# Projection loop turned by three tiles, a new stage for x, and another order behind the last tile

## The reference, cut to what matters

```python
u = rmsnorm(h, norm_mix[i])
z = u @ w_in[i]                                   # 2048 -> 3360 + 3072 + 16
z_rw, z_fox = z[..., :N_SHIFT], z[..., N_SHIFT:]
z_prev = jnp.pad(z_rw, ((0, 0), (1, 0), (0, 0)))[:, :-1]
z_rw = z_rw + (z_prev - z_rw) * mu_shift[i]       # token shift
...
r, k, v, xw, xa, xg = jnp.split(z, RWKV_SPLITS, axis=-1)
w_log = -jax.nn.softplus(-(w0 + jnp.tanh(xw) @ w2)) - 0.5
decay = jnp.exp(-jnp.exp(w_log.astype(f32)))
a = jax.nn.sigmoid(a0 + xa @ a2)
kk = kk / jnp.maximum(jnp.sqrt(jnp.sum(kk * kk, axis=-1, keepdims=True)), 1e-12)
k = k * (1.0 + (a - 1.0) * k_a)
# a scan over 512 steps of a 64x64 state per head, with r, decay, k, v, kk, a
bonus = jnp.sum(r_h * k_h * r_k.astype(f32), axis=-1, keepdims=True) * v_h
...
logits = jnp.einsum('bhqd,bhkd->bhqk', q_blk, kh).astype(f32) * scale
logits = logits + (c_blk[..., None] - c[:, :, None, :])   # causal, per block of 128
probs = jax.nn.softmax(logits, axis=-1)
out = jnp.einsum('bhqk,bhkd->bhqd', probs.astype(vh.dtype), vh)
```

## Time and profile before

| what | value |
|---|---|
| median of 3 runs | 2836.48 us (2836.39 to 2837.19) |
| time of the profiled execution | 2838.68 us |
| its span | 2837.0 us |
| TensorE busy | 2745.4 us (97%) |
| VectorE, ScalarE, GpSimd busy | 1244.4, 882.0, 165.9 us |
| mean granted TensorE clock | 0.981 |
| DMA, mean over the span | 109 GB/s |

### The profile page before, as it was taken

The page is one execution under the profiler, slowest core; times in us unless marked ns, Lnnn a source line. Parts: engine busy times, 40 slices in busy tenths (PEclk is TensorE's granted clock), DMA queues, the critical chain, the costliest instruction groups (busy, mean ns, idle before and its releaser), DMA issues.

```text
span 2837.0 us, 46091 instructions
## 1 busy us (share of the span) xinstructions
PE 2745.4 (97%) x17826; PEld 2190.1 (77%) x17826; DVE 1244.4 (44%) x1635; ACT 882.0 (31%) x1300; POOL 165.9 (6%) x172
## 2 busy tenths in 40 slices
PE   8999999999779899999999999999999999999997
PEld 5867777777458867888888888888888888888886
DVE  4365555665524454544322343223432243334444
ACT  4244444444334432422211222112221122223233
POOL 0000000000023200200000000000000000011110
PEclk9999999999879999999999999999999999999998
DMA  6444555454352233333333333333333333333333
GB/s 183 125 132 141 149 149 145 119 148 130 95 167 93 82 104 89 96 97 96 96 96 96 96 96 96 96 96 96 96 96 96 97 97 97 96 97 105 99 93 91
DMA packets 533117, 309.64 MB, mean 109 GB/s; under 512 B 56365, under 2 KB 508613, under 8 KB 532045
## 3 DMA queue, kind: packets, MB, share of 16 engines
q1 hardware_dynamic: 484093, 275.83, 33.8%
q10 hardware_dynamic: 43552, 14.71, 1.9%
q0 software_dynamic: 5424, 18.45, 1.7%
HBM read 272.64 MB, written 36.31 MB: 109 GB/s over the span
## 4 chain that ended last, share of the span: by engine, by line
issue 56%; PE 36%; DVE 2%; POOL 2%; DMA 2%; ACT 1%; SPq 0%; DVEq 0%; POOLq 0%; ACTq 0%
PE acc L563 6%; PE acc L565 6%; PE acc L564 6%; PE acc L913 2%; PE acc L914 2%; PE acc L915 2%; POOL sumsq L1867 2%; PE bank L647 1%; PE bank L634 1%; PE bank L717 1%; PE bank L727 1%; PE bank L662 1%; PE acc L727 1%; DMA w_raw<-in_w_in 1%; PE bank L640 1%
## 5 line engine op out<-in xcount | busy, mean ns | idle before, releaser
L1405 DVE TENSOR_TENSOR w_lo<-w_raw,w_hi 128x1024 fp32r<-128x1024 f32 (+1 forms) x422 | 522.5, 1238 | 1172.3 <-ACT w_hi L1041 1170.8
L1041 ACT ACTIVATE w_hi<-w_raw 128x1024 fp32r<-128x1024 f32 x420 | 444.8, 1059 | 1225.4 <-PE acc L565 1161.2
L563 PE MATMUL acc<-a_hi,w_hi 128*128 128x512 f32 x1824 | 719.5, 394 | 4.4 <-DVE w_lo L1405 4.3
L565 PE MATMUL acc<-a_hi,w_lo 128*128 128x512 f32 x1824 | 711.6, 390 | 0.0
L564 PE MATMUL acc<-a_lo,w_hi 128*128 128x512 f32 x1824 | 711.4, 390 | 0.0
L563 PE MATMUL acc<-b_hi,w_hi 128*128 128x512 f32 x1280 | 498.5, 389 | 0.0
L565 PE MATMUL acc<-b_hi,w_lo 128*128 128x512 f32 x1280 | 498.0, 389 | 0.0
L564 PE MATMUL acc<-b_lo,w_hi 128*128 128x512 f32 x1280 | 498.0, 389 | 0.0
L563 PEld LDWEIGHTS acc<-a_hi,w_hi 128*128 128x128 f32 x1824 | 343.3, 188 | 89.9 <-issue 18.7
L565 PEld LDWEIGHTS acc<-a_hi,w_lo 128*128 128x128 f32 x1824 | 343.2, 188 | 71.8
L564 PEld LDWEIGHTS acc<-a_lo,w_hi 128*128 128x128 f32 x1824 | 343.3, 188 | 71.1 <-issue 1.7
(11 more groups left out here) (267 smaller groups left out, 2151.2 us busy)
## 6 DMA issues: line engine op xcount, KB each, us to landing
w_raw<-in_w_ff SPq DMA_DIRECT2D x256, 512.0 KB, 4.0
w_raw<-in_w_in SPq DMA_DIRECT2D x100, 512.0 KB, 3.8
w_raw<-in_w_out SPq DMA_DIRECT2D x32, 512.0 KB, 3.9
w_raw<-in_w_ple_gate SPq DMA_DIRECT2D x32, 512.0 KB, 3.9
z_d<-ev POOLq DMA_DIRECT2D x50, 256.0 KB, 3.4
ab_d<-ab ACTq DMA_DIRECT2D x8, 1024.0 KB, 7.0
x_c<-ab_d SPq DMA_DIRECT2D x8, 1024.0 KB, 4.9
x_t<-ab_d SPq DMA_DIRECT2D x9, 512.0 KB, 3.9
```

Of the source, the lines that this page charges most:

```text
L563: mm(dst, wh, hi[:, kt, :], start=kt == 0, stop=False)
L565: last = mm(dst, wl, hi[:, kt, :], start=False, stop=kt == KT - 1)
L1041: A(w_hi[:, s, :, :], w_raw[:, s, :, :], ACT.Copy).then_inc(sg("w_hi_ready"), 1)
L1405: V.tensor_tensor(w_lo[:, s, :, 0:width], w_raw[:, s, :, 0:width], w_hi[:, s, :, 0:width].bitcast(F32), ALU.subtract).then_inc(sg("w_split ...
```

## The change

What it does:

- The order of a pair's tiles is k, q, fox k, fox v, r, v. The loop starts after the third tile of a pair (`Z_LEAD = 3`), so a turn computes fox v, r and v of pair i and k, q, fox k of pair i+1, with the side work of pair i beside them. The last three tiles of the eighth pair come behind the loop with steps 1 to 5 beside them (`last_side`), and the once-only steps stand in the first three tiles.
- `load_pair` loads k, q and fox k, and waits for the store of the third tile of the pair. Fox v, r and v are loaded by themselves, each two tiles after its own.
- Beside the tiles, VectorE's receptance (shift of r) moves from step 2 to 6, the values (shift of v, bonus) from 3 and 7 to 8, the features to 7; ScalarE's store of `ab` moves to step 7, those of v and the bonus to 9. Two operations of VectorE per pair are merged into others. `pr` has a buffer for each head.
- Behind the last tile VectorE does receptance and features first, then values, and head 1's softmax last.
- In the x stage the narrow product is made block by block (`narrow`), its weights have a buffer of their own, the first unit is loaded and split inside the stage, h is stored by quarters as they are ready, and four blocks of squares are added up by four matmuls of 32 columns that write different partitions.

```diff
-Z_COLUMNS = (DR, 0, 2 * DR, N_SHIFT, N_SHIFT + DR, N_SHIFT + 2 * DR)
+Z_COLUMNS = (DR, N_SHIFT, N_SHIFT + DR, N_SHIFT + 2 * DR, 0, 2 * DR)
+Z_LEAD = 3
...
             def load_pair(i):
-                sp.wait_ge(sg("ev_free0"), i * 48 + 80)
+                sp.wait_ge(sg("ev_free0"), i * 48 + 64)
...
-                sp.wait_ge(sg("ev_free1"), i * 48 + 64)
+                sp.wait_ge(sg("ev_free1"), i * 48 + 48)
...
                 sp.wait_ge(sg("side_inputs_used"), i + 1)
-                for t, dst in enumerate((kin, rin, vin, qin, k_in)):
...
+                for t, dst in enumerate((kin[:, 1:], qin[:, :], k_in[:, :])):
+                    load_tile(i, t, dst, "side_landed")
...
             with sp.Fori(0, NPAIR - 1) as i:
                 for t in range(Z_PAIR):
-                    pair_units(i, 2 + Z_PAIR + t, t)
+                    pair_units(i, 2 + Z_LEAD + t, (Z_LEAD + t) % Z_PAIR)
                     if t == 0:
                         load_pair(i)
-                    if t == 1:
+                    if t == 2:
                         load_fox_v(i)
+                    if t == 3:
+                        load_receptance(i)
+                    if t == 4:
+                        load_value(i)
...
-            def sum_squares(f):
-
-                pe.wait_ge(sg("squares_ready"), f + 1)
-                mm(bank[3][:, :], ones, sq[:, f % 2, :], start=f == 0, stop=f == KT - 1).then_inc(sg("x_squares_summed"), 1)
+            def sum_squares(g):
+
+                pe.wait_ge(sg("squares_ready"), NB * g + NB)
+                for j in range(NB):
+                    last = mm(bank[3][32 * j:32 * j + 32, :], const(C_ONE, 32), squares[j], start=g == 0, stop=g == H_X - 1)
+                last.then_inc(sg("x_squares_summed"), 1)
+
+            def narrow(k):
...
+                mm(bank[0][0:48, :], nw_hi[:, k, :], a_hi[:, k, :], start=k == 0, stop=False)
+                mm(bank[0][0:48, :], nw_hi[:, k, :], a_lo[:, k, :], start=False, stop=False)
+                return mm(bank[0][0:48, :], nw_lo[:, k, :], a_hi[:, k, :], start=False, stop=k == KT - 1)
...
+            i = NPAIR - 1
+            pair_tiles(i, 2 + Z_LEAD, last_side, Z_LEAD)
+            pe.wait_ge(sg("logits_max_ready"), i * 8 + 4)
+            logits(i, 1)
+            pe.wait_ge(sg("fv_ready"), i + 1)
+            pe.wait_ge(sg("acc_taken"), 2 + Z_TILES)
+            sum_bonus(i, acc[1])
+            transpose_probs(i, 0, last_prob_banks)
+            weigh_values(i, 0)
+            transpose_probs(i, 1, last_prob_banks)
+            weigh_values(i, 1)
...
+            def store_values(i):
+
+                act.wait_ge(sg("bonus_taken"), i + 1)
+                act.dma_start(v_d[:, :, bass.ds(i, 1), :].rearrange("p c a t -> p c (a t)"), vs[:, :].rearrange("p (c t) -> p c t", c=NC)).then_inc(sg("features_stored"), 16)
+                act.dma_start(bonus_d[bass.ds(i, 1), :, :].rearrange("a p t -> (a p) t"), bon[:, :]).then_inc(sg("features_stored"), 16)
...
                 if at == 7:
+                    store_features(i)
                     take_probs(i, 0)
                 if at == 8:
...
                     exps(i, 1)
                 if at == 9:
                     normalize(i, 1)
+                    store_values(i)
...
+            store_features(i)
+            normalize(i, 0)
+            store_values(i)
+            take_probs(i, 0, last_prob_banks)
+            exps(i, 1)
+            normalize(i, 1)
+            take_probs(i, 1, last_prob_banks)
+            store_fox(i)
...
+            receptance(i)
+            features(i)
+            invert_sums(i, 0)
+            values(i, acc[1])
+            softmax(i, 1)
+            invert_sums(i, 1)
```

More of the change, by code:

```diff
@@ L385, in _ @@
             for s in range(2):
[L386 to L390, removed]
+                unit(s, w_in_v[:, s * UK:(s + 1) * UK, 3 * DR + P:3 * DR + 2 * P], Z_ODD + 2 + s)
             def pair_units(i, m, t):
@@ new lines, in spread_rows, with first_logits @@
+            def spread_rows(i):
+                pe.wait_ge(sg("row_split"), i + 1)
+                for n in range(3):
+                    mm(bank[2 + n][:, :], spread_r[:, n, :], row_hi[0:6, :], start=True, stop=False)
+                    last = mm(bank[2 + n][:, :], spread_r[:, n, :], row_lo[0:6, :], start=False, stop=True)
+                last.then_inc(sg("head_spread"), 1)
+            def first_logits(i):
+                pe.wait_ge(sg("qk_ready"), i * 3 + 3)
+                logits(i, 0)
@@ new lines, in turn_values, with sum_bonus @@
+            def turn_values(i):
+                pe.wait_ge(sg("fv_landed"), i * 16 + 16)
+                for q in range(T // P):
+                    last = nc.tensor.transpose(bank[0][:, q * P:(q + 1) * P], v_in[:, q * P:(q + 1) * P], ident)
+                last.then_inc(sg("fv_done"), 1)
+            def sum_bonus(i, dst=bank[1]):
+                pe.wait_ge(sg("rk_ready"), i + 1)
+                mm(dst[:, :], const(C_BLK, P), t2[:, :], start=True, stop=True).then_inc(sg("bonus_summed"), 1)
@@ L660, in side @@
[L660 to L663, removed]
-                if at == 4:
[L665 to L668, removed]
-                    last.then_inc(sg("head_spread"), 1)
@@ L1047, in next_units, with fold @@
                         between()
-            def fold(hi, gain, f, n, b, gains=True, summed="squares_summed"):
+            def fold(hi, gain, f, n, b, gains=True):
                 act.wait_ge(sg("h_ready"), n + 1)
@@ L1087, in _, with pair_tiles @@
             stage(0, 2)
-            def pair_tiles(i, m, beside):
-                for t in range(Z_PAIR):
+            def pair_tiles(i, m, beside, count=Z_PAIR):
+                for t in range(count):
                     for s in range(2):
@@ L1142, in side @@
[L1142 to L1143 removed]
+                    square_qk(i)
                 if at == 2:
[L1145 to L1148 removed]
@@ L1475, in _, with pair_tiles @@
             stage(0, 2, body=project)
-            def pair_tiles(i, m, beside):
-                for t in range(Z_PAIR):
-                    b = t % 2
+            def pair_tiles(i, m, beside, count=Z_PAIR):
+                for t in range(count):
+                    b = (m + t) % 2
                     for s in range(2):
```

474 lines of the change are left out of this document (290 added, 184 removed).

## The result

The changed kernel takes 2915.76 us (median of 4 runs, 2913.97 to 2916.33) against 2836.43 beside it: ratio 1.028, 95% interval 1.026 to 1.030, 79 us slower. The forecast was 2922. The profiled execution took 2915.31 us, its span 2913.6, which is 76.6 more than before (2837.0).

The account below looks back on a forecast made before the run. TensorE bounds the loop, the chain across engines the stretch behind the last tile. Terms +115 -5.9 +14 -25 -12 = +86 us on 2836.5 give 2922 us, 3% slower; 8-in-10 range 2880 to 2955.

Parts of the forecast that it names:

- stall of a pair, eight times: In the turned loop: late side loads and weights queued behind them delay the next tile 14.4 us a pair, 115 us.
- first turn's old stall: First turn of the loop: its existing 5.9 us loss is already in the new stall and comes off.
- later in a turn: Late steps of a turn: moved stores and receptance behind an eviction cost 2 us a turn, 14 us in seven.
- behind the last tile: From last tile's end to recurrence: last pair's steps 1 to 5 lie under its tiles, gain 25 us.
- x stage: Before tile 0: weights and 48-column product move inside the stage, gain 12 us, ends 4 and 16.
- What I took as one chain: Stall in the loop: store, pair's loads, weights, then squares and head sums in succession, 14.4 us a pair.
- the first rival: Loop: side work starts before the weights count, only the pair's own chain costs, 5 us a pair, 2848; 10 in 100.
- The rival that this wait grows to 6 us: Loop: ScalarE's 5.2 us of issuing comes in full, half clock after it, 6 us a turn, 2950; 8 in 100.
- ScalarE issues v's and the bonus' stores until E + 18.4: Behind the last tile: these stores hold ScalarE until 18.4 us after tile end, ahead of copying head 0's probabilities.
- my end of 30: Behind the last tile: upper end of the gain, 30 us, if the clock stays up.
- My end of 4 for squares one after another: x stage: if the four 32-column squares run serially, TensorE becomes the pacer and the gain is 4 us.
- VectorE paces it: x stage: VectorE's folds and narrow-weight work set the time, tile 0 at 38.5, a gain of 15 us before offsets.

Follow-up runs that it names:

- experiment 2: Changed kernel turned by two tiles instead of three (lead of four): 2817.15 us, ratio 0.993 against the kernel before.
- experiment 1: Changed kernel with the second tile's weights queued ahead of the pair's loads on SyncE's queue: 2882.94 us, ratio 1.016 against the kernel before.
- experiment 4: Kernel before the change, with ScalarE issuing the stores of v and the bonus ahead of the 1 MB store: 2835.36 us, ratio 1.000.
- experiment 5: Kernel with a lead of four tiles, TensorE's bonus sum half a half-tile later: 2811.09 us, ratio 0.992 against the kernel before.
- experiment 3: Changed kernel with full 128 by 128 matmuls replacing the four 32-column ones that sum x's squares: 2922.56 us, ratio 1.030 against the kernel before.
- experiment 9: Kernel with only fox k late, later bonus sum and ScalarE-issued narrow loads, plus the 48-column product one block later on TensorE: 2799.71 us, ratio 0.988.
- two more edits: On the kernel with only fox k loaded late: bonus sum half a half-tile later and narrow loads issued by ScalarE; 2802.01 us, ratio 0.989.
- experiments 1 to 3 and 5 to 9: Includes lead of four with ScalarE-issued narrow loads (2818.16 us), changed kernel with only fox k late (2809.97), and that with two more edits (2802.01).
- experiment 10: Changed kernel with only fox k loaded late, plus the loop's order of steps behind the last tile: 2812.87 us, ratio 0.993 against the kernel before.

## Why the prediction was right, term by term

The spans divide at tile 0, at E of the first and of the last pair, at the last tile's end and at the recurrence:

| term | forecast | measured |
|---|---|---|
| stall of a pair, eight times | +115 (14.4 each) | +105 (13.3 a turn on the mean, 11.8 in the last pair) |
| first turn's old stall | -5.9 | -5.9 |
| later in a turn | +14 (2.0 each) | +10 (1.47 each) |
| last pair's own matmuls, now ahead of the last tile's end | none | +8.5 |
| behind the last tile | -25 | -30.9 |
| x stage | -12 | -8.7 |
| rest | 0 | -1.2 |
| sum | +86 | +77 |

The mean turn is (798.35 - 103.20) / 7 = 99.31 us; less 84.58, less the 1.47 that experiment 2's turn has without a stall, it leaves 13.3. The last pair's 8.5 is 52.95 us from its E to the last tile's end less three tiles of 10.88 and 11.8 of stall.

**The stall** was right in place, releasers and order. Its size was 1.1 to 1.6 too high a pair, mostly since the load starts 1.1 sooner after E. What I took as one chain was two: experiment 1 takes the weights out and 9.3 of 13.3 us stay on the mean. That also refutes the price of the first rival (a short stall, the pair's own chain at 5 us): it reckoned head sums at full clock and a landing at E + 14, and experiment 1 shows 5.2 us of head sums at half clock and a landing at E + 15.6.

**Later in a turn** the sum was near and one of its reasons wrong. ScalarE's issue of v and the bonus, which I priced at 5.2 us, takes 0.39 and 0.47 in the loop:

```profile
582.74 0.39 ACTq L1282 DMA_DIRECT2D v_d<-vs  x1
...
583.29 0.47 ACTq L1283 DMA_DIRECT2D bonus_d<-bon  x1
```

Moved away from the 1 MB store it costs nothing (experiment 4). The 1.47 us is to 0.87 the bonus sum behind VectorE's receptance, which I had named (experiment 5); of the other 0.6, which experiment 5 still has, 0.35 is the wait for ScalarE's copies and the rest wasn't taken apart. The rival that this wait grows to 6 us rested on the same wrong price.

**Behind the last tile** the step that failed is "ScalarE issues v's and the bonus' stores until E + 18.4": counted from the last tile's end they were out at E + 15.1. I had taken 4.2 us as the length of v's issue. What stayed the same is its end, some 4.2 us after the end of the 1 MB store's issue in both kernels (780.63 to 784.88 before, 861.05 to 865.24 here), and the change issues the 1 MB store 2.6 us ahead. Then the second head ran at full clock: from the second reciprocal (870.51) to the recurrence it took 8.1 us, not 10.6. The gain was 31, past my end of 30. Against that stands a term I left out: three tiles can only cover the last pair's steps if its matmuls take TensorE's time there, 8.5 us.

**The x stage** gained 8.7 of 12. The overlap of the four squares was right, and by the Trainium skill's page TensorEngine Tiling (Array Packing), section Key Properties, tiles work independently: the trace agrees, four in 1.07 us. The drain that the same section states for a change of mode has no wait of its own in the trace. It could only lie in the start: behind four transposes that had waited for x the narrow product starts 0.41 us later (31.89 to 32.30), the squares 0.58 (26.87 to 27.45), so I estimate it at 0.2 us or less from these. My end of 4 for squares one after another was too high: experiment 3 leaves 0.9 of the gain (52.6 against 53.4). What failed is "VectorE paces it": the first sum of squares stood behind TensorE's product that waits for nw_lo (experiment 9), and what holds the rest stays open, with waits for x's blocks in the trace.

**The sum** came nearer than its terms. The 8.5 us that I left out and the 3 us too much in the x stage's gain made the kernel slower than I had it, the smaller stall, the cheaper turn and the larger gain behind the last tile made it faster by 20, and the two partly cancel. That part of the closeness of 2922 to 2916 is luck; the stall, its place and its releasers are not.

## What to carry to other kernels

When a loop is turned so that work starts right behind its last input, look in the in-order queue for what waits behind that input's store and doesn't need it. Here one load of seven needed it, and cutting it out turned 79 us of loss into 24 of gain (32 with two more edits). A lead that hides a pair's last steps under tiles also puts their matmuls ahead of the tiles' end; count both. And before a long issue in a trace is priced as that transfer's own, look at what was issued ahead of it.

## What the runs showed of the hardware

- The issue of v's 256 KB store on ScalarE's queue took 4.0 to 4.2 us directly behind that of a 1 MB store and 0.39 in experiment 4 ahead of it, at the same size and pattern. Issued 2.5 to 2.7 us after the 1 MB store's issue it took 1.46 to 1.80 (behind the last tile in the change and in experiments 1 to 3 and 5 to 9), and 9.7 us after it 0.41 (experiment 10). Wherever it took more than 0.43, it ended 4.1 to 4.3 us after the 1 MB store's issue had ended. Two narrow loads on SyncE's queue behind four of x took 5.38 us to issue, and 3.15 when ScalarE issued them first. A queue without room would explain both; only the dependence on the place is shown.
- Four 128 by 32 matmuls of 512 columns, side by side, took 1.07 us at the full granted clock (1.94 in the first block), four full ones 3.7.
- Where TensorE stood for 3.9 and then 7.3 us (the change) or for 4.9 (experiment 1), the granted clock was at 0.5 in the next window, and the head sums took 4.1 and 5.2 us instead of the 2.7 that they took in the trace of before: 1.5 to 2.5 us of each stall.
